# A reordered front and a compression layer that runs over positions outside, in a one-core decoder-layer kernel

## The chip, the cores and the metric

The kernel runs on one core of one Trainium2 chip. The metric is the device time of one execution in microseconds (us). The kernel before took 2623.63 us, the median of three runs (2619.42 to 2636.91).

## The reference

One inference step of a one-layer decoder trunk over 320 tokens: a prompt of 256 tokens and eight samples of eight tokens, all in fp32, width 2048. What is computed, in the order in which it matters here:

```
n    = rmsnorm(x, norm1)
z    = n @ w_in          # q 1024 | 6 x 256 key/value columns | 24 gates | conv b, c, h: 3 x 1024
q, k = rmsnorm per head of 128, times qk_gain
conv = b * (causal convolution, width 3, of c*h, plus bias)
kc, vc = gelu(sum over 32 positions of rows @ w1[position] + pe @ w1) @ w2   # blocks of 32 rows, stride 16
attn = gated sum of compressed, selected and window attention, with a bias by distance
h    = x + concat(rmsnorm(attn), rmsnorm(conv)) @ w_out
h    = h + PEER(rmsnorm(h, norm2))    # 8 heads x 16 experts of 16384, rows gathered from memory
y    = h + sigmoid(rmsnorm(h, norm3) @ w_gate) * (p @ w_p)
```

Outputs are y and the new rows of the caches. One of them, `win_sample`, holds the last 256 rows of each sample's window buffer: 248 old rows, copied unchanged from the input `state_win`, and 8 new ones. The compression has two kinds, 0 for keys and 1 for values, each with its own w1 (4 MB) and w2.

## The kernel before, in words

All of it is written out by hand in one program per engine. SyncE (SP) issues nearly all transfers, in program order, on one queue; where SP waits for a semaphore, all transfers written behind it wait too. GpSimd (POOL) only issues the expert gathers. Semaphores order the rest. One large tensor, `arena`, holds everything in on-chip memory, so every tile carries that name in the profile.

The tokens are three tiles: two of 128 prompt tokens and one of 64 sample tokens. The front (1) loads the constants, x and `norm1`'s gain turned by channel, (2) turns x, 16 chunks of 128 channels for all three tiles, through two PSUM banks (`transposes`, L1642), with VectorE (DVE) evicting the even chunks and ScalarE (ACT) the odd ones, times the gain, into `xT`, and (3) multiplies with `w_in` in twelve blocks of 512 columns (`product`, L1668 and L1673). Blocks 0 to 7 are for tile 0 alone (32 matmul records each), blocks 8 and 9 for all tiles, block 10 the gates, block 11 the window keys and values. The rms factor is applied when a product is evicted.

The weights of a block come as two halves of 2 MB into a ring of four slots. `fill` (L379) waits until a slot's last user is done (`w_used`) and issues the load; `fill_z(blk)` fills both halves. Among these fills the SP program has four other things, each at a fixed place:

- L401: `bias_dram`, a store of eight partitions, each repeated 128 times in rows of 1564 bytes (1564 KB). It is behind block 3's fills. Behind block 5's fills SP waits for it (`bias_out`) and reads it back as `bias_p` and `bias_s` (L409, L411).
- L402: the copy of the 248 old rows of eight samples from `state_win` to the output (3968 KB, memory to memory), right behind L401.
- L419: two copies of `cu`, shifted by one and by two partitions (127 and 126 partitions of 4 KB), for the convolution, behind `u_ready`.
- L421 to L426: the convolution's state, taps and a gain by channel (`chan_in`).

Behind block 11 follows the compression. `raw_rows(kind)` turns the rows of one kind (eight samples' pages, the prompt's rows, and `pe`) through banks 6 and 7, and ACT evicts them (`raw_out`). `first_layer(kind)` (L1732) multiplies 32 positions for each of the two halves `hb` of the hidden units, `hb` outside, 64 products of 285 columns in all. `hidden(kind)` on ACT (L747, L749) makes the gelu of each half. The order on TensorE is `raw_rows(0)`, `first_layer(0)`, `raw_rows(1)`, the second layer of kind 0 (L1745), twelve transposes of heads, `first_layer(1)` and the second layer of kind 1 (L1759). Kind 1's weights go into the same place as kind 0's, when all of `first_layer(0)` is done. SP then stores the new key and value rows (L470 to L474), loads `norm2`, the keys and the first half of `w_out`, and copies the prompt's values to `v_prompt` (L489, 4 x 128 KB), for which `scores(0)` (L1780) and DVE wait (`vp_in`). The attention, the output product, the expert gathers and the last product follow.

Of the kernel before, what the change touches and what calls it, by code (L numbers as in the profile page):

```python
# [9 lines left out]
KC = D // 128  # L10
# [60 lines left out]
def build(nc, I, O):  # L71
# [48 lines left out]
    gT = buf(K0 + NCST, 4, KC)  # L120
    qg = buf(K0 + NCST + 64, 4, HD)
# [100 lines left out]
    v_ready, root_ready = sem("v_ready"), sem("root_ready")  # L222
    t_mm, t_ev = sem("t_mm"), [sem("t_ev_bank6"), sem("t_ev_bank7")]
# [4 lines left out]
    qkv_ready, vn_in = sem("qkv_ready"), sem("vn_in")  # L228
    w1_in, w2_in, pe_in_s, conv_done, u_out = [sem("w1_in0"), sem("w1_in1")], sem("w2_in"), sem("pe_in"), sem("conv_done"), sem("u_out")
# [132 lines left out]
    def _(sp):  # L362
# [27 lines left out]
        for i, name in ((1, "norm2"), (2, "norm3"), (3, "out_gain")):  # L390
            channel_gain(i, name, small_in)
        sp.dma_start(pages[0:1, :], I["page_table"].rearrange("(o b) n -> o (b n)", o=1)).then_inc(small_in, 16)
        sp.dma_start(qg, bass.AP(I["qk_gain"].tensor, 0, [[0, 128], [HD, 4], [1, HD]])).then_inc(small_in, 16)
        sp.dma_start(cw[:, 0:3, :], bass.AP(I["conv_w"].tensor, 0, [[0, 128], [CONV, 3], [1, CONV]])).then_inc(cw_in, 16)
        sp.dma_start(cw[:, 3, :], bass.AP(I["conv_b"].tensor, 0, [[0, 128], [1, CONV]])).then_inc(cw_in, 16)

        for blk in range(2, 4):
# [4 lines left out]
        sp.dma_start(win_s[:, 0:PAST - NT, :], I["state_win"][0].rearrange("b t s g d -> b t (s g d)")[:, NT:, :])\  # L402
          .then_inc(out_done, 16)
        for blk in range(4, 6):
            fill_z(blk)

        sp.wait_ge(bias_out, 16)
        bt = bias_dram.tensor
        sp.dma_start(bias_p, bass.AP(bt, DMAX - 128, [[NBIAS - 1, 128], [128 * NBIAS, NH], [1, 256]])).then_inc(bias_in, 16)  # L409
        for r in range(2 * NH):  # L410
            sp.dma_start(bias_s[NT * r:NT * r + NT, :],  # L411
                         bass.AP(bt, (r % NH) * 128 * NBIAS + DMAX - PAST, [[NBIAS - 1, NT], [1, DMAX + 1]])).then_inc(bias_in, 16)
        for blk in range(6, 9):
            fill_z(blk)
# [3 lines left out]
        for d, dst in ((1, sh1), (2, sh2)):  # L418
            sp.dma_start(dst[d:128, 0, :], cu[0:128 - d, 0, :]).then_inc(shift_a, 16)  # L419
        fill_z(9)  # L420
        sp.dma_start(state_rows[0:2 * NB, :], I["state_conv"][0].rearrange("b w c -> (b w) c")).then_inc(chan_in, 16)  # L421
        with nc.allow_non_contiguous_dma(reason="taps and gains by channel"):
            for w in range(3):
                sp.dma_start(cwT[:, w, :], I["conv_w"][0, w].rearrange("(c p) -> p c", p=128)).then_inc(chan_in, 16)
            sp.dma_start(cwT[:, 3, :], I["conv_b"][0].rearrange("(c p) -> p c", p=128)).then_inc(chan_in, 16)
            sp.dma_start(qg_T, I["qk_gain"][0, 0].rearrange("(p o) -> p o", o=1)).then_inc(chan_in, 16)  # L426
        for blk in range(10, 12):
# [21 lines left out]
        sp.wait_ge(small_in, 16 * 5)  # L449
# [5 lines left out]
        sp.wait_ge(mm_done, 12)  # L455
        compress_weights(0, 1)
        for kind in range(2):
            sp.dma_start(w2[kind], I["cmp_w2"][0, kind].rearrange("(a p) h -> p a h", p=128)).then_inc(w2_in, 16)
            sp.dma_start(pe_in[kind][0:BLK, :], I["cmp_pe"][0, kind]).then_inc(pe_in_s, 16)
        for b in range(NB):  # L460
            sp.wait_ge(t_mm, KC + 1 + b + 1)
            page_rows(1, b)
        sp.wait_ge(cmp_mm, 2)
        compress_weights(1, 0)
# [8 lines left out]
        for b in range(NB):  # L473
            sp.dma_start(win_s[b, PAST - NT:PAST, :], z[b * NT:b * NT + NT, 2, 2048:2560]).then_inc(kv_out, 16)  # L474
        sp.dma_start(g2[0], bass.AP(I["norm2"].tensor, 0, [[0, 128], [1, D]])).then_inc(g2_in, 16)
# [7 lines left out]
        sp.wait_ge(t_mm, KC + 2 * (NB + 2))  # L483
        fill_rows(N_OUT, 0, "out")
        sp.wait_ge(t_mm, KC + 2 * (NB + 2) + 12)
# [188 lines left out]
    def _(act):  # L674
# [18 lines left out]
        act.wait_ge(first_in, 32)  # L693
        odd_transposes(KC, lambda e, c: e.activation(xT[:, c, 0:TOK], bank[7][:, 0:TOK], ACT.Copy, scale=gT[:, 0, c:c + 1]))
# [18 lines left out]
        for part, region in enumerate((bg, cu, sh1)):  # L713
            for j in range(2):
# [100 lines left out]
        act.wait_ge(small_in, 16 * 5)  # L815
# [275 lines left out]
    def _(dve):  # L1091
# [40 lines left out]
        dve.wait_ge(bias_mm, 1)  # L1132
        dve.tensor_copy(bias_row[0:NH, :], bank[0][0:NH, 0:NBIAS]).then_inc(bias_sb, 1)
        dve.wait_ge(first_in, 32)
        even_transposes(KC, lambda e, c: e.tensor_scalar(xT[:, c, 0:TOK], bank[6][:, 0:TOK], gT[:, 0, c:c + 1], None, ALU.mult))
        dve.wait_ge(x_in, 64)
# [5 lines left out]

# [1099 lines left out]
```

## Time and profile before

| | us |
|---|---|
| median of three runs (lowest to highest) | 2623.63 (2619.42 to 2636.91) |
| the profiled execution | 2632.44 |
| its span in the trace | 2630.6 |
| TensorE busy, share of the span | 1712.5, 65% |
| VectorE busy | 1148.4, 44% |
| GpSimd busy | 905.6, 34% |
| ScalarE busy | 332.0, 13% |

Busy times overlap, so they don't add up to the span. An idle engine costs time only where the chain of work that ends last runs through it. All times below are from the start of the span. "Granted clock" is the share of TensorE's full clock that it was given; 1.00 is 2.4 GHz and 0.50 is 1.2 GHz.

### The profile page before, as it was taken

The page shows a single profiled execution, that of the slowest core. Times are in us where ns is not written, and L with a number is a line of the kernel's source. Part 1 is how long each engine was busy: PE and PEld are TensorE (multiplying, and loading weights), DVE is VectorE, ACT ScalarE, POOL GpSimd, SP SyncE. Part 2 cuts the span into 40 slices and gives each one's busy share as a digit, 9 for nine tenths or more (in the row PEclk, how much of TensorE's full clock was granted, in tenths as well). Part 3 has the DMA queues.
Part 4 walks back from the last instruction along what each step waited for, and adds up shares of the span by engine and source line. Part 5 has one row for each costly group of instructions (what it writes and reads, how often), then busy time and mean ns, then how long its engine had stood idle before and what let it go on. Part 6 is the DMA issues. An engine that isn't in the chain of part 4 may idle for free.

```text
span 2630.6 us, 21422 instructions
## 1 busy us (share of the span) xinstructions
PE 1712.5 (65%) x8331; PEld 934.6 (36%) x8331; DVE 1148.4 (44%) x2124; ACT 332.0 (13%) x726; POOL 905.6 (34%) x644
## 2 busy tenths in 40 slices
PE   7599898988898677788678433233233223577677
PEld 3245576487777446533267200000000000122224
DVE  1002112114453764354443466656564775544442
ACT  1000123001000332210110110101101012101002
POOL 0000000003222443322343455665665665655430
PEclk9799896989899676678788666666666665777888
DMA  9683452667999879989999899999999999999996
GB/s 318 209 290 104 141 185 96 223 217 305 396 403 408 322 308 384 361 314 377 376 415 380 355 415 421 421 422 421 422 422 421 421 422 418 396 416 416 415 418 221
DMA packets 228649, 907.12 MB, mean 345 GB/s; under 512 B 29749, under 2 KB 54197, under 8 KB 144614
## 3 DMA queue, kind: packets, MB, share of 16 engines
q0 software_dynamic: 92160, 671.13, 61.9%
q1 hardware_dynamic: 136174, 233.79, 25.5%
q8 instruction: 64, 1.05, 0.2%
q10 hardware_dynamic: 216, 0.86, 0.1%
q14 instruction: 35, 0.29, 0.0%
HBM read 893.70 MB, written 14.52 MB: 345 GB/s over the span
## 4 chain that ended last, share of the span: by engine, by line
DMA 48%; PE 41%; DVE 3%; issue 3%; ACT 2%; POOL 2%; SPq 1%; DVEq 0%; ACTq 0%; PEldq 0%; POOLq 0%
DMA arena<-in_peer_v,arena 30%; PE bank L1668 8%; PE bank L2043 6%; DMA arena<-in_w_in 5%; DMA arena<-in_peer_u,arena 5%; PE bank L2058 5%; DMA arena<-in_peer_wq 3%; PE bank L1732 3%; DMA arena<-in_w_out 2%; PE bank L1860 2%; PE bank L1836 2%; PE bank L1993 2%; PE bank L2163 2%; DMA arena<-in_state_win 2%; PE bank L1973 1%
## 5 line engine op out<-in xcount | busy, mean ns | idle before, releaser
L1465 DVE CUSTOM_DVE_ANT_0 arena<-arena 128x2048 f32<-128x2048 f32 x320 | 731.1, 2292 | 647.3 <-DMA arena<-in_peer_u,arena 643.8
L2043 PE MATMUL bank<-arena 128*32 128x512 f32 x2560 | 461.2, 832 | 661.1 <-DVE arena L1474 501.1
L665 POOL DMA_INDIRECT arena<-in_peer_u,arena x320 | 551.4, 1723 | 879.6 <-DVEq L1444 632.0
L670 POOL DMA_INDIRECT arena<-in_peer_v,arena x320 | 354.0, 1106 | 765.5 <-PE bank L2043 737.3
L2043 PEld LDWEIGHTS bank<-arena 128*32 128x32 f32 x2560 | 69.6, 128 | 1005.9 <-DVE arena L1474 506.8
L1668 PE MATMUL bank<-arena 128*128 128x512 f32 (+2 forms) x544 | 218.3, 562 | 37.4 <-DMA arena<-in_w_in 32.0
L2058 PE MATMUL bank<-arena 128*128 128x192 f32 x1024 | 190.7, 349 | 24.6 <-DMA arena<-in_w_in 23.5
L2058 PEld LDWEIGHTS bank<-arena 128*128 128x128 f32 x1024 | 182.2, 205 | 44.9 <-DMA arena<-in_w_in 29.4
L1668 PEld LDWEIGHTS bank<-arena 128*128 128x128 f32 (+1 forms) x544 | 102.6, 210 | 150.0 <-issue 117.0
L961 ACT ACTIVATE arena<-arena 128x4 f32<-128x4 f32 x80 | 16.8, 211 | 880.0 <-DVE arena L1465 879.8
L2163 PE MATMUL bank<-arena 128*128 128x512 f32 x256 | 117.6, 616 | 0.0
L1993 PE MATMUL bank<-arena 128*128 128x192 f32 x512 | 96.9, 355 | 22.6 <-DMA arena<-in_peer_wq 22.6
L1993 PEld LDWEIGHTS bank<-arena 128*128 128x128 f32 x512 | 93.9, 211 | 28.5 <-DMA arena<-in_peer_wq 24.4
L1472 DVE TENSOR_TENSOR arena<-arena 128x4 f32<-128x4 f32 x80 | 13.1, 163 | 181.6 <-ACT arena L961 180.9
L1973 PE MATMUL bank<-arena 128*128 128x512 f32 x128 | 68.5, 684 | 21.0 <-DMA arena<-in_w_out 21.0
L2163 PEld LDWEIGHTS bank<-arena 128*128 128x128 f32 x256 | 50.2, 200 | 73.4 <-issue 73.4
L1732 PE MATMUL bank<-arena 128*128 128x285 f32 x256 | 66.9, 426 | 1.3 <-ACT arena L738 0.7
L1642 PE MATMUL bank<-arena 128*128 128x128 f32 (+2 forms) x190 | 46.5, 351 | 23.3 <-issue 9.1
L1383 DVE MAX8 arena<-arena 128x8 f32<-128x128 f32 (+1 forms) x120 | 32.5, 326 | 65.7 <-ACT arena L831 63.9
L1860 PE MATMUL bank<-arena 128*128 128x128 f32 x512 | 60.1, 281 | 1.2 <-PE bank L1860 0.6
L1860 PEld LDWEIGHTS bank<-arena 128*128 128x128 f32 x512 | 59.4, 197 | 1.9 <-issue 1.2
L1836 PE MATMUL bank<-arena 128*128 128x512 f32 x128 | 57.4, 608 | 1.0 <-DVE arena L1318 0.5
(245 smaller groups left out, 1532.1 us busy)
## 6 DMA issues: line engine op xcount, KB each, us to landing
arena<-in_w_in SPq DMA_DIRECT2D x22, 2048.0 KB, 13.5
arena<-in_w_in SPq DMA_DIRECT2D x32, 1024.0 KB, 14.8
arena<-in_w_out SPq DMA_DIRECT2D x8, 2048.0 KB, 8.0
arena<-in_peer_wq SPq DMA_DIRECT2D x8, 2048.0 KB, 7.9
arena<-in_w_out SPq DMA_DIRECT2D x16, 1024.0 KB, 14.5
arena<-in_peer_wq SPq DMA_DIRECT2D x16, 1024.0 KB, 23.4
arena<-in_ple_gate SPq DMA_DIRECT2D x32, 512.0 KB, 14.8
arena<-in_ple_gate SPq DMA_DIRECT2D x6, 2048.0 KB, 12.5
```

The source lines that it names most:

```text
L665: pool.indirect_dma_start(u_row[j], None, I["peer_u"][0], bass.IndirectOffsetOnAxis(idx[:, i, c + j:c + j + 1], 0)).then_inc(u_in[j], 16)
L670: pool.indirect_dma_start(v_row[j], None, I["peer_v"][0], bass.IndirectOffsetOnAxis(idx[:, i, c + j:c + j + 1], 0)).then_inc(v_in[j], 16)
L1465: dve.tensor_tensor_reduce(out=u_row[j], in0=u_row[j], in1=rep_of(i), scale=1.0, scalar=0.0, op0=ALU.mult, op1=ALU.add, accum_out=a4[:, pa ...
L1668: ins = pe.matmul(bank[3 * par + t][0:ROWS[t], 0:width], xT[:, 8 * half + k, 128 * t:128 * t + ROWS[t]], ring[slot][:, k, 0:width], start= ...
L1732: ins = pe.matmul(bank[hb][:, 0:(SEQS + 1) * NWIN], w1[:, m, hb * 128:hb * 128 + 128], view, start=(m == 0), stop=(m == BLK - 1))
L1836: ins = pe.matmul(bank[blk][:, :], xT_a[:, 8 * half + k, :], ring[slot][:, k, :], start=(half == 0 and k == 0), stop=(half == 1 and k == 7))
L1860: ins = pe.matmul(bank[4 * (n % 2) + sub][:, 0:128], ring[slot][:, k, 128 * sub:128 * sub + 128], nT_a[:, 8 * half + k, :], start=(half == ...
L1973: pe.matmul(bank[4 + 2 * (blk % 2)][:, :], out_T(4 * q + k, 1), ring_b[ring_of(f)][:, k, :], start=(q == 0 and k == 0), stop=(q == 3 and k ...
L1993: ins = pe.matmul(bank[4 + sub][:, 0:192], ring_b[ring_of(f)][:, k, 128 * sub:128 * sub + 128], nT_b[:, 4 * q + k, :], start=(q == 0 and k ...
L2043: ins = pe.matmul(bank[i % 2][32 * q:32 * q + 32, :], diag[:, k % 2, j, :], v_row[j][:, 512 * q:512 * q + 512], start=(s == 0 and j == 0), ...
L2058: ins = pe.matmul(bank[4 + x][:, 0:192], ring_c[f % 3][:, k, 128 * x:128 * x + 128], xn_T[:, 4 * q + k, :], start=(q == 0 and k == 0), sto ...
L2163: ins = pe.matmul(bank[4 + t][:, :], hT[:, 2 * part + k, 128 * t:128 * t + 128], gate_w[gate_slot(q)][:, k, :], start=(part == 0 and k == ...
```

## The change

`norm1`, `norm2`, `norm3` and `out_gain` are loaded as 64 rows of 128 channels and turned by one TensorE transpose into `gT`, in place of four loads with one descriptor for each number. Tile 0 of x is loaded first and turned alone; the other tiles are loaded behind block 0's weights and turned between blocks 1 and 2. The bias product (L1652) now stands behind tile 0's transposes. On SP the store of `bias_dram` moves behind the two shifted copies, its read-back behind the taps and ahead of block 10's fills, and the copy of `state_win` behind the new key and value rows. In the compression the positions run outside and `hb` inside, `raw_rows(1)` stands behind position 15 of `first_layer(0)`, the first 12 positions' weights are replaced when position 11 is done, the twelve transposes stand ahead of kind 0's second layer, and `pe` is loaded ahead of w1's second piece.

```diff
+        for i, name in enumerate(("norm1", "norm2", "norm3", "out_gain")):
+            sp.dma_start(gain_rows[KC * i:KC * i + KC, :], I[name][0].rearrange("(k p) -> k p", p=128)).then_inc(gains_in, 16)
         sp.dma_start(cst, I["cst"]).then_inc(cst_in, 16)
-        tiles_of(xp, xs, h, x_in)
-        sp.dma_start(h[64:128, 2, :], xs).then_inc(x_in, 16)
+        sp.dma_start(h[:, 0, :], xp[0]).then_inc(x0_in, 16)
...
-        channel_gain(0, "norm1", first_in)
+        fill_z(0)
+        sp.dma_start(h[:, 1, :], xp[1]).then_inc(x_in, 16)
+        sp.dma_start(h[0:64, 2, :], xs).then_inc(x_in, 16)
+        sp.dma_start(h[64:128, 2, :], xs).then_inc(x_in, 16)
         sp.dma_start(tab[0:NBUCKET, :], I["rel_bias"]).then_inc(first_in, 16)
-        for blk in range(2):
-            fill_z(blk)
+        fill_z(1)
...
-        sp.wait_ge(bias_sb, 1)
-        sp.dma_start(bias_dram, rep(bias_row[0:NH, :], [0, 128], [1, NBIAS])).then_inc(bias_out, 16)
-        sp.dma_start(win_s[:, 0:PAST - NT, :], I["state_win"][0]...).then_inc(out_done, 16)
-        for blk in range(4, 6):
-            fill_z(blk)
-        sp.wait_ge(bias_out, 16)
-        ... (bias_p, bias_s)
-        for blk in range(6, 9):
+        for blk in range(4, 9):
             fill_z(blk)
 
         sp.wait_ge(u_ready, 1)
         for d, dst in ((1, sh1), (2, sh2)):
             sp.dma_start(dst[d:128, 0, :], cu[0:128 - d, 0, :]).then_inc(shift_a, 16)
+        sp.wait_ge(bias_sb, 1)
+        sp.dma_start(bias_dram, rep(bias_row[0:NH, :], [0, 128], [1, NBIAS])).then_inc(bias_out, 16)
         fill_z(9)
         ... (state_rows, taps, qg_T)
+        sp.wait_ge(bias_out, 16)
+        ... (bias_p, bias_s)
         for blk in range(10, 12):
             fill_z(blk)
...
+        sp.wait_ge(w1_used, 1)
+        compress_weights(1, 0)
         sp.wait_ge(cmp_mm, 2)
-        compress_weights(1, 0)
         compress_weights(1, 1)
...
+        sp.dma_start(win_s[:, 0:PAST - NT, :], I["state_win"][0]...).then_inc(out_done, 16)
         sp.dma_start(g2[0], ...)
         sp.dma_start(keys_in, ...)
@@ ScalarE
         act.wait_ge(xn_ready, 1)
         raw_out(0)
         root(stats[:, 36:72], stats[:, 72:108])
-        hidden(0)
         act.wait_ge(conv_done, 1)
         act.wait_ge(xn_out, 32)
         raw_out(1)
+        hidden(0)
         odd_transposes(12, heads_out)
@@ TensorE
+        pe.transpose(bank[1][:, 0:4 * KC], gain_rows[0:4 * KC, :], ident[0:4 * KC, 0:4 * KC]).then_inc(gains_mm, 1)
+        pe.wait_ge(x0_in, 16)
+        transposes(KC, tok_tiles(x_tile, (0,)))
+        pe.wait_ge(first_in, 16)
         pe.wait_ge(dve_step, 2)
-        pe.matmul(bank[0][0:NH, 0:NBIAS], tab..., cst...).then_inc(bias_mm, 1)
-        pe.wait_ge(x_in, 64)
-        transposes(KC, tok_tiles(lambda t, c: h[:, t, 128 * c:128 * c + 128]))
+        pe.matmul(bank[2][0:NH, 0:NBIAS], tab..., cst...).then_inc(bias_mm, 1)
         pe.wait_ge(t_ev[0], 8)
         pe.wait_ge(t_ev[1], 8)
...
-        blocks(0, 8, 1)
+        blocks(0, 2, 1)
+        pe.wait_ge(x_in, 48)
+        transposes(KC, tok_tiles(x_tile, (1, 2)))
+        blocks(2, 6, 1)
+        pe.wait_ge(t_ev[0], 16)
+        pe.wait_ge(t_ev[1], 16)
+        pe.wait_ge(bias_sb, 1)
         blocks(8, 2, 2)
...
-            for hb in range(2):
-                if kind:
-                    pe.wait_ge(hid_ready, hb + 1)
-                for m in range(BLK):
+            if kind:
+                pe.wait_ge(hid_ready, 2)
+            for m in range(BLK):
+                ... (waits for w1_in at m = 0 and W1_CUT)
+                for hb in range(2):
                     ins = pe.matmul(bank[hb][:, 0:(SEQS + 1) * NWIN], w1[:, m, hb * 128:hb * 128 + 128], view,
                                     start=(m == 0), stop=(m == BLK - 1))
-                ins.then_inc(cmp_mm, 1)
+                    if m == BLK - 1:
+                        ins.then_inc(cmp_mm, 1)
+                if kind == 0 and m == W1_CUT - 1:
+                    ins.then_inc(w1_used, 1)
+                if kind == 0 and m == STRIDE - 1:
+                    raw_rows(1)
 
-        pe.wait_ge(mm_ev, 2 + 12)
+        pe.wait_ge(mm_ev, 2 + 10)
         raw_rows(0)
         first_layer(0)
-        raw_rows(1)
+        pe.wait_ge(qkv_ready, 1)
+        transposes(12, ...)
         pe.wait_ge(hid_ready, 2)
         ... (kind 0's second layer)
-        pe.wait_ge(qkv_ready, 1)
-        transposes(12, ...)
         first_layer(1)
```

DVE and ACT follow: each evicts the gains or waits for them, then tile 0's chunks of 128 columns, and later the chunks of 192 columns of tiles 1 and 2 (DVE behind the sums of squares and the bias row, ACT behind block 1's eviction).

## Rows read from the trace of the kernel before

**Rows 1.** Timeline of TensorE, front: start, us, instruction, count, idle before and releaser.

```profile
16.14 1.46 PE L1652 MATMUL bank<-arena 33*8 33x391 f32 x2 [16.14 <-DMA arena<-in_rel_bias]
34.30 15.52 PE L1668 MATMUL bank<-arena 128*128 128x512 f32 x32 [0.97 <-issue]
79.41 13.97 PE L1668 MATMUL bank<-arena 128*128 128x512 f32 x32 [0.40 <-PE bank L1668]
125.35 16.08 PE L1668 MATMUL bank<-arena 128*128 128x512 f32 x32 [31.97 <-DMA arena<-in_w_in]
185.57 13.97 PE L1668 MATMUL bank<-arena 128*128 128x512 f32 x32 [0.62 <-PE bank L1668]
221.00 13.97 PE L1668 MATMUL bank<-arena 128*128 128x512 f32 x32 [0.32 <-PE bank L1673]
256.65 0.21 PE L1698 MATMUL bank<-arena 32*128 32x32 f32 x1 [0.55 <-PE bank L1673]
```

**Rows 2.** Timeline of SP's queue: start, us until SP could go on, transfer, count.

```profile
77.38 49.81 SPq L379 DMA_DIRECT2D arena<-in_w_in  x4
171.02 13.78 SPq L419 DMA_DIRECT2D arena<-arena  x2
184.85 15.01 SPq L379 DMA_DIRECT2D arena<-in_w_in  x2
388.79 0.35 SPq L491 DMA_DIRECT2D arena<-in_x_prompt  x1
```

**Rows 3.** Windows: stretch, PE, PEld, DVE, ACT, POOL busy; clock, DMA share, GB/s.

```profile
4.00:6.00 2.00, 0.00 (x0) 0.00 (x0) 0.00 (x0) 0.00 (x0) 0.00 (x0) 1.00 1.04 413
74.00:76.00 2.00, 2.00 (x6) 0.91 (x5) 0.00 (x0) 0.00 (x0) 0.00 (x0) 1.00 0.45 48
98.00:100.00 2.00, 0.00 (x0) 0.00 (x0) 0.00 (x0) 0.00 (x0) 0.00 (x0) 0.50 0.47 49
102.00:104.00 2.00, 0.00 (x0) 0.00 (x0) 0.00 (x0) 0.00 (x0) 0.00 (x0) 0.50 0.59 254
180.00:182.00 2.00, 2.00 (x6) 0.95 (x5) 0.00 (x0) 0.00 (x0) 0.00 (x0) 1.00 0.06 27
```

**Rows 4.** DVE's timeline: the convolution's first group, and who held it.

```profile
203.86 8.78 DVE L1155 TENSOR_TENSOR arena<-arena 128x1024 f32<-128x1024 f32 x7 [43.70 <-DMA arena<-arena]
```

**Rows 5.** Fills of block 9 (L379, issued 184 to 186): issue to landing.

```profile
DMA to landing us min/median/max: 24.8/27.0/29.3
```

**Rows 6.** x's first tile (L366, issued at 1.20): issue to landing.

```profile
DMA to landing us min/median/max: 6.1/6.1/6.1
```

**Rows 7.** First fill of w_in (L379, issued at 14.54): issue to landing.

```profile
DMA to landing us min/median/max: 7.9/7.9/7.9
```

**Rows 8.** Chain of waits, the transposes of three tiles: start, us, what.

```profile
21.39 11.95 PE bank L1642 x39
```

**Rows 9.** Timeline of TensorE, compression: `raw_rows` begins at 314.74 and 358.64.

```profile
314.74 1.06 PE L1642 MATMUL bank<-arena 128*128 128x128 f32 x8 [2.34 <-ACT arena L709]
323.86 0.22 PE L1642 MATMUL bank<-arena 32*128 32x32 f32 x1 [1.23 <-DMA arena<-in_cmp_pe]
324.81 33.99 PE L1732 MATMUL bank<-arena 128*128 128x285 f32 x128 [0.73 <-ACT arena L738]
358.64 1.04 PE L1642 MATMUL bank<-arena 128*128 128x128 f32 x8
374.82 32.89 PE L1732 MATMUL bank<-arena 128*128 128x285 f32 x128 [0.57 <-issue]
418.01 0.49 PE L1780 MATMUL bank<-arena 128*128 128x128 f32 x2 [0.48 <-DVEq L1218]
```

**Rows 10.** Timeline of ACT: `hidden(0)`, first half.

```profile
343.67 1.28 ACT L749 ACT_TABLE_LOAD   x1
344.96 0.49 ACT L749 ACTIVATE arena<-bank,arena 128x270 f32<-128x270 f32 x1
```

**Rows 11.** Window at the start of the first layer of kind 0; columns as in rows 3.

```profile
325.00:330.00 5.00, 5.00 (x11) 3.61 (x12) 3.51 (x15) 1.24 (x2) 0.00 (x0) 0.50 0.35 112
```

More of the change, by code:

```diff
@@ L426, in _ @@
             sp.dma_start(qg_T, I["qk_gain"][0, 0].rearrange("(p o) -> p o", o=1)).then_inc(chan_in, 16)
+        sp.wait_ge(bias_out, 16)
+        bt = bias_dram.tensor
+        sp.dma_start(bias_p, bass.AP(bt, DMAX - 128, [[NBIAS - 1, 128], [128 * NBIAS, NH], [1, 256]])).then_inc(bias_in, 16)
+        for r in range(2 * NH):
+            sp.dma_start(bias_s[NT * r:NT * r + NT, :],
+                         bass.AP(bt, (r % NH) * 128 * NBIAS + DMAX - PAST, [[NBIAS - 1, NT], [1, DMAX + 1]])).then_inc(bias_in, 16)
         for blk in range(10, 12):
@@ L455, in _ @@
         sp.wait_ge(mm_done, 12)
+        for kind in range(2):
+            sp.dma_start(pe_in[kind][0:BLK, :], I["cmp_pe"][0, kind]).then_inc(pe_in_s, 16)
         compress_weights(0, 1)
@@ L474, in _ @@
             sp.dma_start(win_s[b, PAST - NT:PAST, :], z[b * NT:b * NT + NT, 2, 2048:2560]).then_inc(kv_out, 16)
+        sp.dma_start(win_s[:, 0:PAST - NT, :], I["state_win"][0].rearrange("b t s g d -> b t (s g d)")[:, NT:, :])\
+          .then_inc(out_done, 16)
         sp.dma_start(g2[0], bass.AP(I["norm2"].tensor, 0, [[0, 128], [1, D]])).then_inc(g2_in, 16)
@@ L691, in odd_transposes @@
             tcount[0] += n
-        act.wait_ge(first_in, 32)
-        odd_transposes(KC, lambda e, c: e.activation(xT[:, c, 0:TOK], bank[7][:, 0:TOK], ACT.Copy, scale=gT[:, 0, c:c + 1]))
+        act.wait_ge(gains_ev, 1)
+        odd_transposes(KC, lambda e, c: e.activation(xT[:, c, 0:128], bank[7][:, 0:128], ACT.Copy, scale=gT[:, 0, c:c + 1]))
         root(stats[:, 0:3], stats[:, 3:6])
@@ L713, in _ @@
         for part, region in enumerate((bg, cu, sh1)):
+            if part == 1:
+                odd_transposes(KC, lambda e, c: e.activation(xT[:, c, 128:TOK], bank[7][:, 128:TOK], ACT.Copy, scale=gT[:, 0, c:c + 1]))
             for j in range(2):
@@ L1644, in transposes, with tok_tiles, x_tile @@
                 evs[par] += 1
-        def tok_tiles(src, rows=ROWS):
-            return lambda c: [(128 * t, src(t, c)[0:rows[t], :], rows[t]) for t in range(3)]
+        def tok_tiles(src, tiles=(0, 1, 2)):
+            return lambda c: [(128 * t, src(t, c)[0:ROWS[t], :], ROWS[t]) for t in tiles]
+        def x_tile(t, c):
+            return h[:, t, 128 * c:128 * c + 128]
         pe.wait_ge(cst_in, 16)
-        pe.wait_ge(first_in, 32)
+        pe.wait_ge(gains_in, 64)
+        pe.transpose(bank[1][:, 0:4 * KC], gain_rows[0:4 * KC, :], ident[0:4 * KC, 0:4 * KC]).then_inc(gains_mm, 1)
+        pe.wait_ge(x0_in, 16)
+        transposes(KC, tok_tiles(x_tile, (0,)))
+        pe.wait_ge(first_in, 16)
         pe.wait_ge(dve_step, 2)
-        pe.matmul(bank[0][0:NH, 0:NBIAS], tab[0:NBUCKET + 1, :], cst[0:NBUCKET + 1, C_OH:C_OH + NBIAS],
+        pe.matmul(bank[2][0:NH, 0:NBIAS], tab[0:NBUCKET + 1, :], cst[0:NBUCKET + 1, C_OH:C_OH + NBIAS],
                   start=True, stop=True).then_inc(bias_mm, 1)
-        pe.wait_ge(x_in, 64)
-        transposes(KC, tok_tiles(lambda t, c: h[:, t, 128 * c:128 * c + 128]))
         pe.wait_ge(t_ev[0], 8)
         pe.wait_ge(t_ev[1], 8)
-        pe.wait_ge(bias_sb, 1)
         def product(done, f, par, tiles, width=512):
@@ L1747, in _ @@
         ins.then_inc(kc_mm, 1)
-        pe.wait_ge(qkv_ready, 1)
-        transposes(12, lambda c: tok_tiles(lambda t, c: z[:, t, TBLOCKS[c]:TBLOCKS[c] + 128])(c)[0:1 if c < NH else 3])
         first_layer(1)
```

56 lines of the change are left out of this document (25 added, 31 removed).

## The prediction, made blind

> **What bounds the kernel now.** I read TensorE's timeline of the front first. It shows blocks of products back to back, 13.97 us each when warm, with three flaws: nothing is multiplied before 34.30; TensorE then stands 31.97 us for `w_in` ahead of block 4 (125.35); and the block behind that gap takes 16.08 instead of 13.97, as the first one does with 15.52 [rows 1]. So the front is bound by TensorE, except for the start and one hole of 32.0 + 2.1 = 34.1 us. The SP queue's timeline and the windows say what the hole is. From 74 to 100 only 0.45 to 0.47 of the transfer engines work, at 48 to 49 GB/s: the store of the bias rows, on about half of the sixteen. Then the copy of `state_win` runs on about half of them too, at 254 GB/s [rows 3]. The two did not run side by side on different halves, so both took the same engines, and block 4's weights, issued at 77.38, waited there for their share [rows 2]. Behind the front, the chain runs through TensorE and later through the gathers. Nothing there is loaded by the clock of the front; all of it waits for earlier work of its own, so what the front and the compression gain or lose passes to the end one for one.
>
> **The start.** Tile 0 landed at 1.20 + 6.1 = 7.3 [rows 6]. Four loads are now issued ahead of it, at 0.35 us or somewhat more each (the shortest issue shown [rows 2]), some 2 us: 9.3. Turning tile 0 and the gains is no longer what block 0 waits for. The bias product stands ahead of block 0, and its table is loaded behind block 0's 4.2 MB and 2.1 MB of x. These 6.3 MB take 15 us at the 413 GB/s of [rows 3] and 24 us at the pace of one half block, 2.1 MB in 7.9 [rows 7]; that row holds the start-up of a first transfer, so I stay near the lower end, 16.5. The table is there at 25.8 and the product takes 1.46 [rows 1]: block 0 starts at 27.3 instead of 34.3, **-7.0** (between -8 and 0). The sixteen transposes of tile 0 lie in the wait for it; without that cover they would cost some 8 us. The loads of gains with one descriptor per number go, and what is late in their place is the table.
>
> **Two tiles turned later.** Before, 39 transposes took 11.95 [rows 8], 0.31 each. Tiles 1 and 2 need 2 x 16, 9.8 us, and TensorE first waits some 0.7 us for ACT's eviction of block 1. A block behind such a stretch took 15.52 instead of 13.97 [rows 1]: 9.8 + 0.7 + 1.6 = **+12.1** (9 to 15).
>
> **The old hole.** Store and copy are no longer ahead of block 4's fills: **-34.1**. Blocks 2 to 7 take 14 us each for 4.2 MB, 300 GB/s, below the 413 that the engines give, so no wait comes back there. Block 8 starts at 185.57 - 7.0 + 12.1 - 34.1 = 156.6.
>
> **The store in its new place.** It is behind the two shifted copies, ahead of block 9's fills. SP reaches the shifted copies at 171.02, when block 6 ends, and block 9 starts at 221.00 [rows 1, 2]: the fills have 50.0 us. Now what was ahead of them before. The copy of 127 partitions ran at 27 GB/s and a share of 0.06 [rows 3]: one engine of sixteen. It held SP 13.78 us [rows 2] and DVE until 203.86 [rows 4], 32.8 us behind the end of block 6. Block 9's first half, issued at 184.85, landed 24.8 us later [rows 5], at 209.7: 5.8 us behind the end of that copy. So a fill is as late as its share on the slowest engine, and the slack is 11.3 us. The store adds its time on every engine that it uses: 1564 KB at 49 GB/s are 32.7, and the stretch seen is from about 71 to 100; I take 30. Does it use the engine of the shifted copies? Store and `state_win` copy chose the same engines out of sixteen, so the choice does not rotate; I take it to begin at the same engine each time. Then block 9's first half is there 32.8 + 30 + 5.8 = 68.6 us behind the end of block 6, and block 9 could start at 50.0: a new hole of 18.6. The shifted copy may end a little earlier without fills beside it, so 18, and 2.1 for the slow first block behind a wait of this kind [rows 1]: **+20** (0 if the engines differ: 13.8 + 30 + 5.8 = 49.6, just in time; 31 if the store's other engines start only when the shared one has taken its share).
>
> The Trainium skill, "DMA: Bandwidth & Descriptors", section "Why a DMA increments its semaphore by 16 and not by 1", says that a transfer from SP takes the largest number of engines up to 16 that divides its outer dimension, and the lowest-numbered ones. By that rule 127 partitions go to engine 0 and 8 go to engines 0 to 7, which share engine 0. The trace agrees with the counts (0.06 and 0.47 of sixteen); that the sets overlap no row shows. By the rule the term is 20, without it 0.
>
> The bias rows are read back behind that, and nobody needs them before the attention. The taps (`chan_in`) and block 10's small fills stand behind block 9's fills and are due when block 9 ends, 35.6 us after it starts [rows 1]. I cost these at nothing; should the read-back hold them past block 9, it costs its excess. `pages` and the other small loads lie in SP's waits for slots.
>
> **The compression.** The products are the same 64 + 64, and `raw_rows(1)` costs TensorE the same in the middle as behind. `pe` is loaded earlier: -1.2 [rows 9]. Banks 6 and 7 are filled while ACT still evicts block 11, where TensorE waited 2.34: -0.8 of it, as ACT remains the next in line. Both halves `hb` end together, so ACT makes the table load and both gelus behind the last product, 1.28 + 2 x 0.49 and two small copies [rows 10], 2.7 us; before, half of this lay beside products. Once it delays the odd head transposes, +1.6, once kind 1's second layer, +1.9. The clock is 0.50 at the start of the first layer behind ten us of transposes [rows 11]; the 16.2 us between 358.64 and 374.82 become two stretches of 8 to 9, which may keep it: -1.5 (0 to -3). That replacing weights earlier gains nothing is in [rows 9]: `first_layer(1)` waited 0.57, for no load. Sum **0** (-4 to +4).
>
> **The `state_win` copy** now stands ahead of the prompt's values. SP went on behind them at 388.79 [rows 2]; TensorE needs them at 418.01 [rows 9]. `first_layer(0)` ends about 8 later, and the copy takes 4.06 MB at 254 GB/s, 16 us, up to 20: 413 to 417. Half of kind 1's weights (1.5 MB, 4 us) are no longer ahead: 409 to 413. I take **0**, with 5 to 9 us of slack.
>
> **Sum**: -7.0 + 12.1 - 34.1 + 20 + 0 + 0 = -9. The profiled execution took 2632.4 (span 2630.6), so 2623.4 there; it stands 8.8 above the median of the runs, so the forecast is 2623.6 - 9 = **2615**.
>
> **Rivals.**
> - *The store is hidden* (22%): the shifted copies and the store use different engines, or the store is much faster when it has an engine of its own. For it: 49.6 against 50.0. Against: the fixed choice seen for the two eightfold transfers. -9 - 20 + 2 for a margin that is none = -27: 2597.
> - *The store holds the fills longer* (13%): SP and the seven other engines wait until the shared one can take its descriptors, as SP stood 13.78 us behind the first shifted copy. +11: 2626.
> - *The prompt's values come late, and the kernel is slower* (12%): at `scores(0)` both TensorE and DVE wait for `vp_in`. It decides from 418 on, 5 to 9 us above my estimate; every microsecond beyond costs one, and the clock 2 more. For it: a copy from memory to memory was never timed alone, and between 74 and 100 half the engines moved only 49 GB/s. At 100 GB/s it takes 40 us: landing at 435, 17 + 5 = +22 on -9: +13, 2637.
> - *Something else in it is small or late by a few us* (3%), within the range.
>
> The forecast itself has 50%, with 2608 to 2623 for its own range (start 3, hole 4, compression 4). The range that holds 8 in 10 reaches to the hidden store and to the longer hole: 2594 to 2632. A measurement of this kernel can tell about 1% (26 us) from no change. Faster by over 1% is most of the hidden store, 0.16; slower by over 1% needs values later than at 100 GB/s, 0.05; the rest is 0.79.
>
> **What would show it.** Block 0 starts near 27, behind the bias product, and tile 0's transposes end some 8 us ahead of it. Transposes stand between blocks 1 and 2 for 10 us. There is no wait for `w_in` ahead of block 4, block 8 starts near 157, and one wait of 18 us for `w_in` stands ahead of block 9, with a block of 16 us behind it; in it the transfer engines are nearly idle at a share of 0.06. The first products of the attention wait for nothing. The prediction is wrong if block 9 follows block 8 at once (then the gain is near 27), or if `scores(0)` waits for a transfer.

## The result

The changed kernel took 2616.89 us (median of 20 runs, 2610.11 to 2623.89), the kernel before 2633.59 (median of 20, 2619.38 to 2636.98). The ratio is 0.9947, 95% interval 0.9935 to 0.9960: 14 us faster (10.5 to 17), within 1%; the medians differ by 16.7. The three runs known at the time of the forecast had a median ten below that of the twenty, so the forecast is better judged by its difference, -9, than by its 2615. That difference has the right sign and is too small. The profiled execution of the changed kernel took 2621.77 (span 2620.0), against 2632.44.

| | before | after |
|---|---|---|
| block 0 starts | 34.30 | 29.40 |
| block 4 starts | 125.35 | 101.31 |
| block 8 starts | 185.57 | 159.67 |
| wait for `w_in` ahead of block 9 | none | 8.87 |
| blocks 0 to 9 are done (first small transposes) | 256.65 | 241.20 |
| the attention's first product | 418.01 | 402.60 |
| from there to the end of the span | 2212.6 | 2217.4 |

TensorE's timeline of the changed kernel, the rows that answer to [rows 1] and [rows 8]. The columns are start, duration, instruction, count, and the idle time before it with what ended it.

```profile
28.00 1.47 PE L1662 MATMUL bank<-arena 33*8 33x391 f32 x2 [10.15 <-DMA arena<-in_rel_bias]
29.40 15.96 PE L1675 MATMUL bank<-arena 128*128 128x512 f32 x32
45.67 13.97 PE L1675 MATMUL bank<-arena 128*128 128x512 f32 x32 [0.30 <-PE bank L1675]
60.22 9.82 PE L1644 MATMUL bank<-arena 128*128 128x128 f32 x32 [0.58 <-PE bank L1675]
69.98 16.15 PE L1675 MATMUL bank<-arena 128*128 128x512 f32 x32
86.53 13.97 PE L1675 MATMUL bank<-arena 128*128 128x512 f32 x32 [0.40 <-PE bank L1675]
...
159.67 13.97 PE L1675 MATMUL bank<-arena 128*128 128x512 f32 x32 [0.76 <-PE bank L1675]
...
203.65 15.86 PE L1675 MATMUL bank<-arena 128*128 128x512 f32 x32 [8.87 <-DMA arena<-in_w_in]
```

The hole of 32 us is gone from its place. The bias product, and block 0 behind it, waits 10.15 us for the bias table, the transposes of two tiles stand between the blocks 1 and 2, and a smaller hole stands ahead of block 9, with a slow block behind it.

SP's queue of the changed kernel, to be read against [rows 2]: start, time until SP could go on.

```profile
144.95 13.62 SPq L405 DMA_DIRECT2D arena<-arena  x2
158.62 2.86 SPq L407 DMA_DIRECT2D bias_rows<-arena  x1
161.52 30.74 SPq L380 DMA_DIRECT2D arena<-in_w_in  x2
...
365.35 20.03 SPq L487 DMA_DIRECT2D arena<-arena  x4
393.19 0.35 SPq L489 DMA_DIRECT2D arena<-in_x_prompt  x1
```

The shifted copies hold SP 13.6 us as before, the store is issued at 158.62, and block 9's fills behind it hold SP for 30.74. SP went on behind the prompt's values (L487) at 393.19, so they had landed by then, 9.4 us ahead of the attention.

Windows of the changed kernel, columns as in [rows 3]; what matters is the last two, share of the transfer engines and GB/s. DVE's first group of the convolution, as in [rows 4], follows.

```profile
154.00:158.00 4.00, 4.00 (x11) 1.82 (x10) 0.00 (x0) 0.00 (x0) 0.00 (x0) 1.00 0.06 27
164.00:168.00 4.00, 4.00 (x11) 1.81 (x10) 0.00 (x0) 0.00 (x0) 0.00 (x0) 1.00 0.47 75
172.00:176.00 4.00, 4.00 (x27) 2.01 (x26) 1.38 (x2) 0.00 (x0) 0.00 (x0) 1.00 0.46 55
176.00:180.00 4.00, 4.00 (x19) 1.96 (x16) 3.90 (x4) 0.00 (x0) 0.00 (x0) 1.00 0.47 50
196.00:198.00 2.00, 0.00 (x0) 0.00 (x0) 0.00 (x0) 1.01 (x3) 0.00 (x0) 0.81 0.99 336
202.00:204.00 2.00, 0.35 (x1) 0.38 (x2) 0.00 (x0) 0.00 (x0) 0.00 (x0) 0.50 0.47 178
```

```profile
174.58 8.79 DVE L1157 TENSOR_TENSOR arena<-arena 128x1024 f32<-128x1024 f32 x7 [40.56 <-DMA arena<-arena]
```

The shifted copy alone uses 0.06 of the engines at 27 GB/s. From 164 to 168 the store has begun as well: 75 GB/s, yet the share is 0.47, no more than the store's own [rows 3]. With an engine of its own the copy would have made it 0.53. So it sits on one of the store's eight, and seven of them work on the store until the copy ends, ahead of 174.58.

One sign of the forecast did not come: it had the transfer engines nearly idle (0.06) during the wait ahead of block 9. That wait runs from 194.78 to 203.65, and they are at 0.99 in it at first and still at 0.47 at its end. The store's eight shares say why. In the trace their semaphore steps come within 0.6 us of each other in the kernel before (100.70 to 101.29), but at 186.03, 194.97, 195.25, 195.79 and four times between 197.78 and 197.88 here. So not one engine alone was last: half of the store's engines were.

### The profile page after: what moved, and what is told of

It reads as the page before. It is cut to its first block, busy times and chain, and to the rows that moved or that the text cites. A ratio compares the mean times of both kernels' runs of the same rounds, so it can differ in the third digit from the quotient of the medians.

```text
span 2620.0 us, 21441 instructions
## 1 busy us (share of the span) xinstructions
PE 1715.0 (65%) x8332; PEld 940.3 (36%) x8332; DVE 1150.2 (44%) x2133; ACT 334.0 (13%) x734; POOL 903.9 (34%) x644
## 4 chain that ended last, share of the span: by engine, by line
DMA 48%; PE 39%; issue 3%; DVE 3%; POOL 3%; ACT 3%; SPq 1%; DVEq 0%; ACTq 0%; PEldq 0%; POOLq 0%
DMA arena<-in_peer_v,arena 30%; PE bank L1675 7%; DMA arena<-in_w_in 6%; PE bank L2060 5%; PE bank L2075 5%; DMA arena<-in_peer_u,arena 5%; DMA arena<-in_w_out 3%; DMA arena<-in_peer_wq 3%; PE bank L1745 2%; DMA arena<-in_state_win 2%; PE bank L1877 2%; PE bank L1853 2%; PE bank L2010 2%; PE bank L2180 2%; POOL arena L668 1%
## 5 line engine op out<-in xcount | busy, mean ns | idle before, releaser
L2060 PE MATMUL bank<-arena 128*32 128x512 f32 x2560 | 453.1, 818 | 660.4 <-DVE arena L1476 504.6
L663 POOL DMA_INDIRECT arena<-in_peer_u,arena x320 | 541.4, 1692 | 863.1 <-DVEq L1446 618.0
L668 POOL DMA_INDIRECT arena<-in_peer_v,arena x320 | 362.2, 1132 | 774.9 <-PE bank L2060 744.2
L2075 PEld LDWEIGHTS bank<-arena 128*128 128x128 f32 x1024 | 183.9, 207 | 48.0 <-DMA arena<-in_w_in 34.3
L2180 PE MATMUL bank<-arena 128*128 128x512 f32 x256 | 123.9, 643 | 0.0
L2010 PEld LDWEIGHTS bank<-arena 128*128 128x128 f32 x512 | 95.3, 213 | 26.6 <-DMA arena<-in_peer_wq 22.4
L1990 PE MATMUL bank<-arena 128*128 128x512 f32 x128 | 66.5, 668 | 25.5 <-DMA arena<-in_w_out 25.5
L2180 PEld LDWEIGHTS bank<-arena 128*128 128x128 f32 x256 | 52.7, 209 | 77.2 <-issue 77.2
L1877 PEld LDWEIGHTS bank<-arena 128*128 128x128 f32 x512 | 59.9, 199 | 2.0 <-issue 1.3
L1853 PE MATMUL bank<-arena 128*128 128x512 f32 x128 | 58.5, 616 | 1.0 <-DVE arena L1320 0.5
```

The source lines that it names most:

```text
L663: pool.indirect_dma_start(u_row[j], None, I["peer_u"][0], bass.IndirectOffsetOnAxis(idx[:, i, c + j:c + j + 1], 0)).then_inc(u_in[j], 16)
L668: pool.indirect_dma_start(v_row[j], None, I["peer_v"][0], bass.IndirectOffsetOnAxis(idx[:, i, c + j:c + j + 1], 0)).then_inc(v_in[j], 16)
L1853: ins = pe.matmul(bank[blk][:, :], xT_a[:, 8 * half + k, :], ring[slot][:, k, :], start=(half == 0 and k == 0), stop=(half == 1 and k == 7))
L1877: ins = pe.matmul(bank[4 * (n % 2) + sub][:, 0:128], ring[slot][:, k, 128 * sub:128 * sub + 128], nT_a[:, 8 * half + k, :], start=(half == ...
L1990: pe.matmul(bank[4 + 2 * (blk % 2)][:, :], out_T(4 * q + k, 1), ring_b[ring_of(f)][:, k, :], start=(q == 0 and k == 0), stop=(q == 3 and k ...
L2010: ins = pe.matmul(bank[4 + sub][:, 0:192], ring_b[ring_of(f)][:, k, 128 * sub:128 * sub + 128], nT_b[:, 4 * q + k, :], start=(q == 0 and k ...
```

## The experiments

The landmark in all of them is the attention's first product, 402.60 in the changed kernel. Behind it the span goes on for 2207.6 to 2221.8 us in the thirteen profiles (these two and the eleven below), 2212.6 and 2212.7 in the two of the kernel before; so a difference of 5 us in the front can't be told from one execution's time, but can be from its rows.

**e1: the shifted copies are no longer confined to one engine.**

```diff
-            sp.dma_start(dst[d:128, 0, :], cu[0:128 - d, 0, :]).then_inc(shift_a, 16)
+            sp.dma_start(dst[d:d + 112, 0, :], cu[0:112, 0, :]).then_inc(shift_a, 16)
+            sp.dma_start(dst[d + 112:128, 0, :], cu[112:128 - d, 0, :]).then_inc(shift_a, 16)
```

> The changed kernel, but each of the two shifted copies (127 and 126 partitions) is issued as two: 112 partitions and the remaining 15 or 14. Nothing else differs. Theory (the shifted copy of 127 partitions and the first eighth of the bias store stand one behind the other on the same transfer engine): with no copy confined to one engine, all eight shares of the store start some 4 us behind the end of block 6 and are done 30 us later, so block 9's first half lands about 42 us behind that end and is due after 50. The wait of 8.9 us ahead of block 9 goes, the slow block behind it too: the attention starts 10.8 us earlier, at 392. Rival (the two use different engines, and the store by itself is what block 9 waits for): the wait of 8.9 us stays, the attention starts at 403.

Measured: ratio 0.9922 (0.9893 to 0.9951) to the kernel before, which by itself can't be told from the change's 0.9947; the attention starts at 393.43. SP's queue, a window and TensorE's block 9 of this kernel:

```profile
149.21 0.76 SPq L408 DMA_DIRECT2D bias_rows<-arena  x1
153.22 27.46 SPq L380 DMA_DIRECT2D arena<-in_w_in  x2
```

```profile
172.00:176.00 4.00, 4.00 (x19) 1.86 (x19) 0.00 (x0) 0.00 (x0) 0.00 (x0) 1.00 0.46 49
```

```profile
196.24 13.97 PE L1676 MATMUL bank<-arena 128*128 128x512 f32 x32 [0.31 <-PE bank L1681]
393.43 0.49 PE L1798 MATMUL bank<-arena 128*128 128x128 f32 x2 [0.48 <-DVEq L1221]
```

The wait and the slow block are gone, though the store is written in the same place and runs at 49 GB/s as before. So the confined copy makes the wait. The edit takes away two things at once, though: the shared engine, and the 13.6 us for which SP stood behind the copy. The store is issued at 149.21 instead of 158.62. In the trace its packets (1564 bytes each) run from 156.6 to 187.5 here and from 162.1 to 197.5 in the changed kernel; counted from the start of block 7 (146.09 and 144.94), that is 10.5 to 41.4 against 17.2 to 52.6. Of the 11.2 us that the store ended later, 6.7 are a later begin (SP's wait) and 4.5 a longer run (35.4 instead of 30.9), which I put down to the engine that joined late. The rival with different engines would not have kept the wait in this run either (10.5 + 30.9 + 6 us is about 47 behind block 6, and the fill is due at 50); it falls by the window above, 75 GB/s at a share of 0.47.

**e2: all of x is turned ahead of block 0.** On SP `h[:, 1]`, `h[:, 2]` and the table move ahead of `fill_z(0)`; on TensorE:

```diff
         transposes(KC, tok_tiles(x_tile, (0,)))
+        pe.wait_ge(x_in, 48)
+        transposes(KC, tok_tiles(x_tile, (1, 2)))
...
-        blocks(0, 2, 1)
-        pe.wait_ge(x_in, 48)
-        transposes(KC, tok_tiles(x_tile, (1, 2)))
-        blocks(2, 6, 1)
...
+        blocks(0, 8, 1)
```

> The changed kernel, but all of x and the bias table are loaded ahead of block 0's weights, and the tiles 1 and 2 are turned right behind tile 0, ahead of block 0, as DVE's and ScalarE's evictions are. The gains are still loaded as rows. Theory (what the new start gains is the gains' loading and tile 0 ahead of the rest; turning the other tiles between blocks 1 and 2 costs 10.4 us and a slow block of 16.15 us, 2.2 more, and frees TensorE only for a wait for the table): block 0 starts near 29, as in the changed kernel, and the 12.6 us between the blocks 1 and 2 go; the wait ahead of block 9 stays at 8.9. The attention starts at 390. Rival (TensorE is held by the arrival of weights in the first blocks, so that the turning lay in a wait for them): a wait for weights of up to 10 us shows ahead of block 1 or 2, and the attention starts at 400 or later.

Measured: ratio 0.9929 (0.9901 to 0.9958), by itself not to be told from the change's; the attention at 392.00. TensorE's timeline:

```profile
17.34 11.54 PE L1643 MATMUL bank<-arena 128*128 128x128 f32 x33 [0.24 <-ACT arena L692]
28.81 1.47 PE L1663 MATMUL bank<-arena 33*8 33x391 f32 x2
30.21 15.76 PE L1676 MATMUL bank<-arena 128*128 128x512 f32 x32
46.37 13.97 PE L1676 MATMUL bank<-arena 128*128 128x512 f32 x32 [0.40 <-PE bank L1676]
61.13 14.00 PE L1676 MATMUL bank<-arena 128*128 128x512 f32 x32 [0.79 <-PE bank L1676]
```

Block 0 starts 0.8 later than in the changed kernel, with all three tiles turned instead of one. The turning fits into the wait for the table, and the 12.6 us between the blocks 1 and 2 are saved but for 2.

**e3 and e4: one of the two moved transfers alone, in the kernel before.** e3 moves L401 and its read-back (L409, L411) to where the changed kernel has them; e4 moves L402.

> The kernel before, with one part of the change: the bias store and its read-back stand where the changed kernel has them. The copy of state_win stays behind block 3's weights. Theory (the hole of 32 us ahead of block 4 is the store, then the copy, on the same eight engines): the copy alone takes 16 to 19 us on them, from 72 to about 91, block 4's first half lands at 96 and was due at 93.8, so 2 to 4 us of the 32 remain; a new wait of about 9 us stands ahead of block 9. The attention starts at 418 - 34 + 4 + 11 = 399. Rival (the copy is what fills the hole, the store is cheap): 15 us or more of the hole remain.

> The kernel before, with one part of the change: the copy of state_win stands behind the new key and value rows. The bias store and its read-back stay. Theory: the store occupies eight engines from 71 to 100, block 4's first half lands at 106, due at 93.8: a wait of 12 us and a slow block remain of 34, the attention starts at 418 - 20 = 398. The copy in its new place makes the prompt's values land about 15 us later, still ahead of the attention. Rival (the store is hidden by itself, the copy makes the whole hole): no wait ahead of block 4.

Measured, one run each: e3 2604.29, the attention at 393.64; e4 2608.12, the attention at 397.94. Their waits for weights in TensorE's timeline, first e3's two, then e4's one:

```profile
97.48 15.70 PE L1668 MATMUL bank<-arena 128*128 128x512 f32 x32 [2.93 <-DMA arena<-in_w_in]
200.47 15.56 PE L1668 MATMUL bank<-arena 128*128 128x512 f32 x32 [7.99 <-DMA arena<-in_w_in]
```

```profile
109.49 16.77 PE L1668 MATMUL bank<-arena 128*128 128x512 f32 x32 [14.18 <-DMA arena<-in_w_in]
```

Of the 32 us, 14.2 stay with the store alone in front and 2.9 with the copy alone: together they are one queue of about 30 + 16 us on eight engines. That only what exceeds TensorE's 14 us per block shows is my reading of the three numbers. e3 is 5 us under its expectation at the attention, 4 of them in the stretch below. It reaches the attention 9 us ahead of the whole change.

**e7: the new start alone, in the kernel before.** Store, copy of `state_win` and compression stay as they were.

> The kernel before with one part of the change: the new start (gains as rows, tile 0 first, the others turned between the blocks 1 and 2, the table behind x). The bias store and the copy of state_win stay behind block 3's weights, the compression stays. Theory (the start costs TensorE 7.7 us, but the hole ahead of block 4 ends by the time at which block 1 frees its slots, 4.6 us earlier than before): block 3 ends at 100.5 instead of 93.4, the hole shrinks from 32 to about 20, block 4 starts near 120.7 and the attention at 413.4: faster by 4.6, though the same start costs 7.7 where the hole is gone. Rival (the start is worth the same everywhere): the attention starts at 425.7.

Measured: ratio 1.0014 (0.9993 to 1.0036), no difference. The attention starts at 412.93, which the expectation met for a wrong reason: block 4 starts at 125.89, not 120.7.

```profile
125.89 16.97 PE L1675 MATMUL bank<-arena 128*128 128x512 f32 x32 [25.68 <-DMA arena<-in_w_in]
```

The start lets block 1 end at 59.5, but in the new order the 2 MB of taps stand directly ahead of the store and it gets to the engines no earlier (their share is down to that of the store alone, 0.46 to 0.48, from 76 on, and from 72 in the kernel before). The hole ends when it ended and only swallows the turning. The whole front is a draw: 312.3 at the end of block 11, against 312.4. The 5 us at the attention arise behind it.

**e8: the bias table first.** One line moved, `tab` ahead of `fill_z(0)`.

> The changed kernel with one transfer moved: the bias table (1 KB) is loaded ahead of block 0's weights. Theory (block 0 waits 10.1 us for the table, and nothing else is late): block 0 starts near 19.5 and the attention at 392.5. Rival (behind the table the weights are late): block 0 or 1 waits for w_in, and the attention starts at 398 or later.

Measured, one run: 2611.76; block 0 starts at 19.33, no wait for `w_in` until block 9, the attention at 391.71.

```profile
17.93 1.47 PE L1662 MATMUL bank<-arena 33*8 33x391 f32 x2
19.33 15.86 PE L1675 MATMUL bank<-arena 128*128 128x512 f32 x32
```

A table of 1 KB, queued behind 6.3 MB, held the kernel for 10 us. This and e2 are two ways to use the same wait.

**e6: the compression as before, in the changed kernel.**

> The changed kernel with the compression as before: hb outside, raw_rows(1) behind first_layer(0), both pieces of kind 1's weights behind it, the heads' transposes behind kind 0's second layer, pe behind w1. The front stays. Theory (the compression's part moves nothing: its savings of 2 to 3 us are given back by the gelus of both halves behind the last product, 1.5 and 1.9 us of waits): the attention starts at 402 to 404. Rival (the compression's part gains and the front lost as much): the attention starts 4 us or more later than 402.6.

Measured: ratio 0.9951 (0.9928 to 0.9973), not to be told from the change's own; the attention at 397.22, 5.4 us earlier than in the changed kernel. The expectation was wrong: the old order is the shorter one. From the end of block 11 to the attention's first product:

| order of the compression | us in each profile |
|---|---|
| old, kernel before (two profiles) | 105.6, 105.8 |
| old, in e3, e4, e6, e7, e9 | 101.9, 102.3, 102.3, 100.7, 100.7 |
| new, in the changed kernel, e1, e2, e5, e8 | 107.3, 107.4, 107.4, 107.4, 106.9 |
| new, hb outside for kind 1 only (e10) | 106.3 |

TensorE's timeline of the two first layers, new order in the changed kernel, then old order in e6:

```profile
307.15 18.62 PE L1745 MATMUL bank<-arena 128*128 128x285 f32 x64 [1.10 <-ACT arena L735]
...
333.82 15.63 PE L1745 MATMUL bank<-arena 128*128 128x285 f32 x64
...
351.77 0.44 PE L1644 MATMUL bank<-arena 128*128 128x128 f32 x2 [1.50 <-ACT arena L754]
...
356.37 2.87 PE L1764 MATMUL bank<-arena 128*90 128x128 f32 x12
359.03 31.90 PE L1745 MATMUL bank<-arena 128*128 128x285 f32 x128
...
393.08 8.03 PE L1776 MATMUL bank<-arena 128*15 128x128 f32 x72 [1.92 <-ACT arena L749]
```

```profile
308.17 30.96 PE L1743 MATMUL bank<-arena 128*128 128x285 f32 x128 [1.09 <-ACT arena L736]
...
347.23 1.55 PE L1756 MATMUL bank<-arena 128*90 128x128 f32 x12
...
354.42 32.51 PE L1743 MATMUL bank<-arena 128*128 128x285 f32 x128 [0.57 <-DVE arena L1191]
387.70 8.03 PE L1770 MATMUL bank<-arena 128*15 128x128 f32 x72 [0.55 <-ACT arena L747]
```

The new order waits 1.50 for ACT at the heads and 1.92 instead of 0.55 ahead of kind 1's second layer; kind 0's second layer takes 2.87 instead of 1.55; and kind 0's first layer took 18.62 + 15.63 = 34.3 in its two parts, 32.6 in e1, instead of 30.96.

The granted clock says where the longer products come from. Windows of the changed kernel, columns as in [rows 3]:

```profile
306.90:313.00 6.10, 5.85 (x13) 4.21 (x14) 4.16 (x17) 1.67 (x3) 0.00 (x0) 0.50 0.46 146
354.00:360.00 6.00, 6.00 (x24) 4.55 (x25) 1.66 (x6) 2.16 (x3) 0.00 (x0) 0.52 1.06 360
```

The first six microseconds of kind 0's first layer run at 0.50, which costs the 3 us. The second stretch at 0.50 takes in the heads' transposes, kind 0's second layer (2.87) and the start of kind 1's first layer (31.90).

**e10: hb outside for kind 1 alone.** In `first_layer(1)` the order is hb, then position; `first_layer(0)` is as in the change.

> The changed kernel, with hb outside the positions again in first_layer(1) alone; first_layer(0) keeps the positions outside and raw_rows(1) inside. Theory (3 of the 5 us are the end of first_layer(1): ScalarE makes the table load and both gelus behind the last product, TensorE waits 1.9 instead of 0.5 us and runs the second layer slower for it): the stretch from the end of block 11 to the attention takes 104 to 105 instead of 107.3. Rival (the loss is the alternation of the two halves on TensorE itself): the first layer of kind 1 gets shorter than 30.9, and the wait behind it stays.

Measured, one run: 2624.66; the stretch takes 106.3. The wait ahead of the second layer is 0.55 as in the old order, and the first layer still takes 31.82. So the theory has the wait right (1.4 us) and the sum wrong: I had counted a slower second layer, 9.70 in e1 and e5, that the changed kernel's own profile (8.03) doesn't show. It is the clock again: 0.64 from 382.2 to 387 in e1, 1.00 from 393 to 398 in the changed kernel.

**e11: the kernel before, profiled again.**

> The kernel before, unchanged, profiled a second time. Theory (its first profile showed a slow stretch by chance of the clock: 33.99 us for first_layer(0), where four kernels with the same order took 30.96 to 32.65): the stretch from the end of block 11 to the attention takes 101 to 103 instead of 105.6, while the hole ahead of block 4 is again 32 us. Rival (the position of the stretch in the old front makes it slow): 105 or more.

Measured, one run: 2633.39, the hole 32.4, the stretch 105.8. The theory falls as far as two profiles can tell: both show the slow stretch, and the same order took 100.7 to 102.3 in five kernels with other fronts.

```profile
326.05 33.71 PE L1732 MATMUL bank<-arena 128*128 128x285 f32 x128 [0.73 <-ACT arena L738]
```

The rival of this run, the place of the stretch in the old front, falls too, by e7: block 11 ends there at 312.3, as in the kernel before (312.4), behind a hole that ends within 0.6 us of the same time, and the stretch takes 100.7. The whole difference of 5.0 us is in the two first layers (33.99 + 32.89 against 30.96 + 30.96), and it is the clock's. First e7, then the kernel before (which is at 0.50 from 325 to 330, [rows 11]):

```profile
318.00:323.00 5.00, 4.45 (x19) 2.90 (x17) 4.39 (x12) 4.37 (x6) 0.00 (x0) 0.50 1.10 344
325.50:330.50 5.00, 5.00 (x21) 4.00 (x22) 3.38 (x14) 1.37 (x2) 0.00 (x0) 1.00 0.35 110
```

```profile
316.00:323.00 7.00, 4.60 (x28) 2.93 (x28) 6.44 (x14) 7.00 (x9) 0.00 (x0) 1.00 1.07 347
```

In e7 the clock is at 0.50 during the transposes of `raw_rows(0)`, which wait for ACT's evictions anyway, and back at 1.00 for the first layer; in the kernel before it falls some 8 us later and the products pay. Why it falls later there, in the same transposes, stays open.

**e5 and e9: towards a better version.** e5 is e1 and e2 together; e9 is e5 with the old compression.

> The changed kernel with the edits of both timed runs before: shifted copies issued as 112 + 15 and 112 + 14 partitions, and all of x turned ahead of block 0. Theory (the wait ahead of block 9 and the turning between the blocks 1 and 2 are independent): the attention starts at 402.6 - 9.2 - 10.6 = 382.8, and the kernel takes 0.985 to 0.990 of the kernel before. Rival (with block 8 ten us earlier relative to nothing else, another transfer becomes late): a wait for w_in ahead of block 9 or 10, the attention starts at 390 or later.

> The kernel of e5 (shifted copies split, all of x turned ahead of block 0) with the compression as it was before the change. From the end of block 11 to the attention's first product the kernels with the old order took 105.6, 101.9, 102.3, 102.3 and 100.7 us, those with the new order 107.3, 107.4, 107.4, 107.4 and 106.9. Theory (the new order of the compression costs 5 us on TensorE): the stretch takes 101 to 103, the attention starts at 378 instead of 383.3, the kernel takes 0.985 of the kernel before. Rival (the shorter stretches are chance of the clock): the stretch takes 105 or more.

Measured: e5 2594.58 (2588.27 to 2596.95), ratio 0.9865 (0.9836 to 0.9893), the attention at 383.26, no wait for `w_in` in the front. e9 2594.50 (2589.15 to 2599.22), ratio 0.9855 (0.9831 to 0.9879), the attention at 373.81, the stretch 100.7. Both gains of e1 and e2 add up (9.2 + 10.6 = 19.8 forecast, 19.3 measured at the attention). That the old compression adds to them is shown at the attention, 9.5 us earlier than e5 (6.7 of it in the stretch, the rest in the front ahead of it, which is the same code), but not in the time, where the two intervals overlap. Both are faster than either kernel, by 1.3 to 1.5% than the one before.

## Why the prediction was right, and where it was off

That the median (2616.89) came within 2 us of the forecast 2615 is luck: the kernel before was ten slower than the three runs had said, and the medians differ by 8 more than forecast. By its own steps:

| step | forecast | measured in the changed kernel's profile |
|---|---|---|
| start | -7.0 | -4.9 (block 0 at 29.40) |
| two tiles turned later | +12.1 | +12.6 (10.4 between the blocks, 2.2 for the slow one) |
| the old hole | -34.1 | gone |
| block 8 starts | 156.6 | 159.67 |
| the store in its new place | +20 | +10.8 (8.87 and 1.9) |
| blocks 10 and 11 | 0 | -1.7 (54.1 instead of 55.8) |
| compression | 0 | +1.7 against the kernel before, +5 against the old order in the same front |
| the `state_win` copy | 0, slack 5 to 9 | 0, slack 9.4 |
| sum | -9 | -15.4 at the attention, -10.6 in the profiled spans, -14 in the ratio |

**The mechanism was right for the two transfers.** The store and the copy were the hole (e3, e4), the shifted copy and the store do meet on one engine (75 GB/s at a share of 0.47), the confined copy makes the new wait (e1), and the kernel gained 14 us of the 34 that the old hole was worth. The Trainium skill, "DMA: Bandwidth & Descriptors", section "Why a DMA increments its semaphore by 16 and not by 1", has the rule that I could not read from a row: the largest number of engines up to 16 that divides the outer dimension on both sides, and the lowest-numbered ones. This case agrees: 0.47 for eight partitions with or without the copy of 127 beside it, and the wait gone when 127 became 112 + 15. It shows that the two share an engine, not which numbers the engines have.

**The term that was mis-sized is "the store in its new place"**, 20 forecast and 10.8 measured. I counted 32.8 + 30 + 5.8 = 68.6 us from the end of block 6 (144.94) to block 9's first half. It landed at 203.5, 58.6 behind it. The shifted copy was over by 174.58, 29.6 instead of 32.8: no fills ran beside it. The store's last packet ended at 197.5, so what was left of the store behind the copy took at most 23 us, not the 30 that all eight engines take together, and the fill came 6.0 behind it. The chain on one engine was also too simple a picture: half of the store's engines were last together, and the engines were busy in the wait. The store moved 75 - 27 = 48 GB/s on seven engines and 50 on eight, so an engine stores somewhat faster when fewer others do; that alone doesn't make 23 of 30, and why the late share was so short stays open.

**The start** gained 2 us less as the table landed at 28.0, not 25.8: the 6.3 MB ahead of it came at about 350 GB/s. **The compression's zero** was nearly right (+1.7) only against the kernel before, whose stretch is slow in both of its profiles. The two waits for ACT were forecast as 1.6 and 1.9 and are 1.5 and 1.4. What failed is the -1.5 for the clock: cut into parts, the first layer of kind 0 got slower, not faster (32.6 to 34.3 against 30.96 in e6), and so did kind 0's second layer, both at a granted clock of 0.50. The kernel before has 105.7 in that stretch, and five others with the same code 100.7 to 102.3, because its clock falls later and onto the products (e7 and [rows 11]); what makes it fall later is not shown.

**Whether the parts are worth having**: moving the two transfers is the whole gain. The new start is a draw where the old hole covers the turning (e7); where it doesn't, it costs 7.7 by the rows (12.6 - 4.9), though no run has both moves with the old start. The compression's part costs 5 at the attention in the same front (e6). That is why e3, one of the moves alone, reaches the attention ahead of the full change.

## What to carry to other kernels

When a transfer is moved out of the way of one deadline, list what each transfer engine, not the queue, still holds ahead of the next one, and when the queue can issue it. Here a copy of 127 partitions sat on one engine (share 0.06), held SP for 13.6 us and made the weights behind it late; cut into 112 + 15 it did neither. Work that is turned or evicted early belongs into a wait that exists anyway, so look first for what that wait is for: here it was 1 KB behind 6.3 MB. And before a few microseconds are read out of a stretch, compare it with several profiles that have the same code there, and look at the granted clock: the same products took 30.96 or 33.99 us as the six microseconds at 0.50 fell beside them or into them.

## What was not expected of the hardware

- A first layer of 64 products of 285 columns took 30.96 us at best in the old order and up to 33.99, with the same instructions, waits and data. The difference is where the granted clock stood at 0.50: during the transposes ahead of it in e7 (318 to 323), in the first 5 us of the layer in the kernel before [rows 11].
- Behind the shifted copy the rest of the store took at most 23 us (174.58 to 197.5), where the eight engines together took 30. Its eight shares, which landed within 0.6 us of each other in the kernel before, were spread over 11.9 us.
- SP went on behind a copy of 127 partitions on one engine only after 13.6 us, and behind the store with the fills of block 9 after 30.7, although other engines were free (0.47 busy from 164 to 180). That SP's limit is what is outstanding on the fullest engine is my reading; no run measured it.
